# First g and v products by pairs of token tiles, with the parameters turned among them, in a one-core hybrid encoder kernel

## The reference, cut to what matters

```python
xn = rms_norm(x, pre_g)                          # per token, gain pre_g
u  = einsum('btd,de->bte', xn, w_in)             # 1024 -> 5120 columns
xr, gr, cv_v, cv_g, gc = split(u, 5)             # 1024 columns each: x, gr, v, g, gc below
xr = causal_dwconv(xr, rg_buf, rg_cw, rg_cb)     # width 4
hr = rg_lru(xr, rg_h, wa, ba, wx, bx, lam)       # gates, then h = a*h + b over the tokens
y_r = hr * silu(gr)
v  = cv_v * sigmoid(cv_g)                        # the first thing made from u: g, then v
v  = causal_dwconv(v, cv_buf, cv_cw, cv_cb)      # width 31
v  = silu(layer_norm(v, cv_lg, cv_lb))
y_c = (einsum(v, cv_w2) + cv_b2) * silu(gc)
y  = einsum(concat([y_r, y_c]), w_out)           # 2048 -> 1024
out = x + rms_norm(y, post_g)
```

## Time and profile before

| what | value |
|---|---|
| median of the runs | 809.05 us |
| span of the profiled execution, first to last instruction | 806.3 us |
| TensorE busy (PE) | 783.2 us, 97% |
| VectorE busy (DVE) | 665.5 us, 83% |
| ScalarE busy (ACT) | 422.1 us, 52% |
| GpSimd busy (POOL) | 384.9 us, 48% |
| DMA engines | 32.5% on the main queue |

### The profile page before, as it was taken

How to read it: one execution, slowest core, us unless ns; L and a number is a source line. 1 busy time by engine, 2 the same in 40 slices (tenths; PEclk the granted TensorE clock), 3 DMA queues, 4 the chain that set the end, 5 groups by cost and what they waited for, 6 DMA issues and landing times. The chain is left out here.

```text
span 806.3 us, 12690 instructions
## 1 busy us (share of the span) xinstructions
PE 783.2 (97%) x5158; PEld 763.0 (95%) x5158; DVE 665.5 (83%) x564; ACT 422.1 (52%) x657; POOL 384.9 (48%) x215
## 2 busy tenths in 40 slices
PE   5999999999999999999999999999999799999996
PEld 4899999999999999999999989999999799999995
DVE  5589999999998986986995988982438899799894
ACT  6522374474474365365366379953515244566652
POOL 4325347346546446456556744010036896389220
PEclk9999999999999999999999999999999999999998
DMA  8311211211211121121121120423279463554683
GB/s 269 96 54 37 70 53 53 80 52 53 73 59 52 58 73 52 53 79 52 53 79 52 53 80 27 134 71 116 80 240 279 142 171 107 157 157 132 187 262 139
DMA packets 111404, 82.37 MB, mean 102 GB/s; under 512 B 3179, under 2 KB 101483, under 8 KB 111362
## 3 DMA queue, kind: packets, MB, share of 16 engines
q1 hardware_dynamic: 110432, 80.68, 32.5%
q0 software_dynamic: 928, 1.12, 0.6%
q10 hardware_dynamic: 2, 0.00, 0.0%
HBM read 68.55 MB, written 13.25 MB: 101 GB/s over the span
## 5 line engine op out<-in xcount | busy, mean ns | idle before, releaser
L919 PE MATMUL ps<-act_hi,w_hi 128*128 128x352 f32 (+4 forms) x1384 | 445.1, 322 | 5.6 <-DVE w_lo L2067 4.2
L921 PE MATMUL ps<-act_hi,w_lo 128*128 128x352 f32 (+4 forms) x1384 | 438.6, 317 | 0.0
L920 PE MATMUL ps<-act_lo,w_hi 128*128 128x352 f32 (+3 forms) x1320 | 420.2, 318 | 0.0
L1870 DVE SCALAR_TENSOR_TENSOR ps<-cv_in,par_cv,ps 128x1086 f32<-128x1086 f32 x232 | 313.9, 1353 | 7.8
L919 PEld LDWEIGHTS ps<-act_hi,w_hi 128*128 128x128 f32 x1384 | 260.5, 188 | 12.7 <-issue 7.2
L921 PEld LDWEIGHTS ps<-act_hi,w_lo 128*128 128x128 f32 x1384 | 261.1, 189 | 0.0
L920 PEld LDWEIGHTS ps<-act_lo,w_hi 128*128 128x128 f32 x1320 | 248.1, 188 | 0.2
L721 POOL TENSOR_TENSOR w_lo<-wstage,w_hi 128x1024 fp32r<-128x1024 f32 x40 | 97.3, 2447 | 74.7 <-ACT w_hi L1272 74.6
L920 PE MATMUL ps<-act_hi,w_hi 128*128 128x264 f32 (+2 forms) x256 | 73.7, 288 | 0.0
L1272 ACT ACTIVATE w_hi<-wstage 128x1024 fp32r<-128x1024 f32 x47 | 48.6, 1052 | 22.4 <-PE ps L921 15.4
L919 PE MATMUL ps<-act_lo,w_hi 128*128 128x264 f32 x192 | 55.5, 289 | 0.0
(11 more groups left out here) (241 smaller groups left out, 1048.5 us busy)
## 6 DMA issues: line engine op xcount, KB each, us to landing
wstage<-in_w_in SPq DMA_DIRECT2D x40, 512.0 KB, 3.9
wstage<-in_w_out SPq DMA_DIRECT2D x20, 512.0 KB, 5.0
w_stage<-in_w_out SPq DMA_DIRECT2D x19, 512.0 KB, 5.0
stage<-in_w_out SPq DMA_DIRECT2D x9, 512.0 KB, 4.1
silu_spill<-silu_gc SPq DMA_DIRECT2D x8, 528.0 KB, 2.7
yr_spill<-y_rg SPq DMA_DIRECT2D x8, 528.0 KB, 2.8
silu_l<-silu_spill SPq DMA_DIRECT2D x8, 528.0 KB, 3.7
yr<-yr_spill SPq DMA_DIRECT2D x2, 2112.0 KB, 11.1
```

What stands on the lines that cost most here:

```text
L919: pe.matmul(out, wh, xh, start=start, stop=False)
L920: pe.matmul(out, wh, xl, start=False, stop=False)
L921: return pe.matmul(out, wl, xh, start=False, stop=stop)
L1870: STT(out=acc, in0=src, scalar=w, in1=acc, op0=ALU.mult, op1=ALU.add).then_inc(taps, 1)
```

## The change

Section g of the first tile is no longer done in three chunks over 358, 358 and 356 tokens, but in four parts over 256, 256, 256 and 304 tokens (`FIRST_G`; the first two share one bank). The first chunk of v stands between the second and the third part of g. The turns of token tiles 4 to 8 stand at other steps. The parameters are turned ahead of g's last part. POOL makes both parts of the second weight block, ahead of the parameter loads. The gain row is copied once by DVE from PSUM to SBUF, and the norms of token tiles 4 to 8 read it there, which frees PSUM banks 6 and 7. TensorE does twelve products of the identity by a constant into banks that nobody reads (`keep_busy`), three, two, one and six, ahead of the turns of tiles 0 to 3. ACT's table for tanh and exp is loaded ahead of the first tanh, and the first tanh and the first v input are taken in smaller pieces.

```diff
@@ -82,9 +82,11 @@
 BANK = {"g": [2, 3, 4], "v": [0, 1, 2], "gr": [3, 4, 0], "x": [1, 2, 3], "gc": [4, 0, 1]}
 GATE_BANK = [(4, 0), (0, 1), (1, 2)]
 ACC_BANK = 5
-FIRST_BANK = {"g": [4, 5, 6], "v": [1, 2, 3]}
+FIRST_BANK = {"g": [6, 4, 5], "v": [7, 2, 3]}
+FIRST_G = [(0, 4 * P), (4 * P, 2 * P), (6 * P, T - 6 * P)]
 X_BANK = [0, 2, 4, 0, 2, 0, 2, 0, 2]
 GAIN_BANK = 6
+PSUM_GAINS = 4
 
 
 LAST_BANK = {"gr6": [2, 3, 4], "x": [2, 3, 4], "gc": [0, 1, 5], "gr": [0, 1, 6]}
@@ -295,6 +297,7 @@
     assert 4 * D <= 4 * R_LEN
     par_rows = at("par_rows", [D], F32, arena)
     sq_junk = at("sq_junk", [D], F32, arena + 4 * R_LEN)
+    gain = at("gain", [D], F32, arena + 2 * 4 * R_LEN)
 
 
 
@@ -373,6 +376,7 @@
         g_loaded = sem("g_loaded")
         ones_set = sem("ones_set")
         gain_spread = sem("gain_spread")
+        gain_set = sem("gain_set")
         par_loaded = sem("par_loaded")
         gatew_loaded = sem("gatew_loaded")
         consts = sem("consts")
@@ -818,9 +822,10 @@
                     pool.dma_start(par_rows[row:row + src.shape[0], :], src).then_inc(par_loaded, 16)
 
 
-            pool.wait_ge(w_loaded[0], 16)
-            pool.tensor_copy(WHI[0], wstage[:, 0]).then_inc(w_his, 1)
-            w_lo_part(0, 0, 1)
+            for slot in range(2):
+                pool.wait_ge(w_loaded[slot], 16)
+                pool.tensor_copy(WHI[slot], wstage[:, slot]).then_inc(w_his, 1)
+                w_lo_part(slot, slot, slot + 1)
             load_par(par_src)
 
 
@@ -832,7 +837,6 @@
                 for b in range(2):
                     pool.dma_start(gate_w[64 * b:64 * b + 64, (m + b) % 2],
                                    w[0].rearrange("(c b) i j -> b i c j", b=2)[b]).then_inc(gatew_loaded, 16)
-            w_lo_part(1, 1, 2)
 
             pool.wait_ge(par_turned, 1)
             pool.memset(rg_in[:, 0:RPAD], 0.0).then_inc(pads, 1)
@@ -920,7 +924,17 @@
                 pe.matmul(out, wh, xl, start=False, stop=False)
                 return pe.matmul(out, wl, xh, start=False, stop=stop)
 
-            def chunk(s, j, bank=None, between={}):
+            def first_part(s, bank, b0, c0, n, between={}):
+
+                w = WSLOT[s]
+                for k in range(KT):
+                    mm = product(ps[:, bank, b0:b0 + n], WHI[w][:, k], WLO[w][:, k],
+                                 act_hi[:, k, c0:c0 + n], act_lo[:, k, c0:c0 + n], k == 0, k == KT - 1)
+                    if k in between:
+                        turn_x(between[k])
+                return mm
+
+            def chunk(s, j, bank=None):
 
                 bank = BANK[s][j] if bank is None else bank
                 c0, n = (META + j * OCH, OCH) if s in ("gr", "gc") else XCH[j]
@@ -928,8 +942,6 @@
                 for k in range(KT):
                     mm = product(ps[:, bank, 0:n], WHI[w][:, k], WLO[w][:, k],
                                  act_hi[:, k, c0:c0 + n], act_lo[:, k, c0:c0 + n], k == 0, k == KT - 1)
-                    if k in between:
-                        turn_x(between[k])
                 mm.then_inc(proj, 1)
 
             def turn_x(t):
@@ -1030,22 +1042,42 @@
                                start=True, stop=True)
             mm.then_inc(gain_spread, 1)
             pe.wait_ge(consts, 5)
-            for t in range(4):
-                turn_x(t)
+            def keep_busy(bank, n):
+
+                for _ in range(n):
+                    pe.matmul(ps[:, bank, 0:P], ident[:, :], mean_w[:, :], start=True, stop=True)
+
+            keep_busy(4, 3)
+            turn_x(0)
+            keep_busy(4, 2)
+            turn_x(1)
+            keep_busy(4, 1)
+            turn_x(2)
+            pe.wait_ge(x_lo, 1)
+            keep_busy(0, 6)
+            turn_x(3)
+            pe.wait_ge(gain_set, 1)
+            bank = FIRST_BANK["g"]
             pe.wait_ge(w_los, 1)
-            for j, between in enumerate(({0: 4, 2: 5, 5: 6}, {1: 8}, {})):
-                if j == 1:
-                    turn_x(7)
-                pe.wait_ge(x_lo, 3 * j + 3)
-                chunk("g", j, FIRST_BANK["g"][j], between=between)
+            pe.wait_ge(x_lo, 2)
+            first_part("g", bank[0], 0, 0, 2 * P)
+            turn_x(4)
+            pe.wait_ge(x_lo, 4)
+            first_part("g", bank[0], 2 * P, 2 * P, 2 * P, {3: 5}).then_inc(proj, 1)
+            pe.wait_ge(w_los, 2)
+            first_part("v", FIRST_BANK["v"][0], 0, *XCH[0], {1: 6, 6: 7}).then_inc(proj, 1)
+            pe.wait_ge(x_lo, 6)
+            first_part("g", bank[1], 0, *FIRST_G[1], {0: 8}).then_inc(proj, 1)
 
             pe.wait_ge(par_loaded, 16 * (len(par_src) + 2))
+            pe.wait_ge(x_lo, 8)
             for k in range(KT):
-                mm = pe.transpose(ps[:, 7 * (k // 4), k % 4 * P:k % 4 * P + PAR],
+                mm = pe.transpose(ps[:, k // 4, k % 4 * P:k % 4 * P + PAR],
                                   par_rows[0:PAR, k * P:(k + 1) * P], ident[0:PAR, 0:PAR])
             mm.then_inc(par_turned, 1)
-            pe.wait_ge(w_los, 2)
-            for j in range(3):
+            pe.wait_ge(x_lo, NX)
+            first_part("g", bank[2], 0, *FIRST_G[2]).then_inc(proj, 1)
+            for j in range(1, 3):
                 chunk("v", j, FIRST_BANK["v"][j])
             tile(0, True)
             with pe.Fori(1, KT - 1) as c:
@@ -1304,25 +1336,33 @@
                 x_stats(t)
                 x_hi_part(t - 1)
             x_hi_part(NX - 1)
-            act.wait_ge(w_los, 1)
-            act.wait_ge(w_loaded[1], 16)
-            w_hi_part(1, 1)
+            def first_tanh(j, done):
+                c0, n = FIRST_G[j]
+                act.wait_ge(proj, done)
+                return A(tanh_g[:, c0:c0 + n], ps[:, FIRST_BANK["g"][j], 0:n], ACT.Tanh, scale=0.5)
+
+            act.preload_act_table(ACT.Exp)
+            first_tanh(0, 1)
+            first_tanh(1, 3).then_inc(g_read, 1)
             act.wait_ge(par_turned, 1)
             for i in range(2):
                 A(par[:, 4 * i:4 * i + 4, 0:PAR],
-                  ps[:, 7 * i, :].rearrange("p (k n) -> p k n", n=P)[:, :, 0:PAR], ACT.Copy).then_inc(par_ready, 1)
+                  ps[:, i, :].rearrange("p (k n) -> p k n", n=P)[:, :, 0:PAR], ACT.Copy).then_inc(par_ready, 1)
 
             act.wait_ge(der, 2)
             A(small[:, 1, :], small[:, 1, :], ACT.Exp, scale=-1.0).then_inc(der_exp, 1)
+            act.wait_ge(w_los, 2)
+            act.wait_ge(w_loaded[0], 32)
+            act.wait_ge(proj, 4)
+            w_hi_part(0, 0)
+            first_tanh(2, 4).then_inc(g_read, 1)
 
             def gate_tanh(d):
 
-                fst = isinstance(d, int) and d == 0
-                n = 0 if fst else 6 if isinstance(d, int) and d == 1 else d * (3 * NS) - 12
-                bank = (FIRST_BANK if fst else BANK)["g"][0]
+                n = 6 if isinstance(d, int) and d == 1 else d * (3 * NS) - 12
+                bank = BANK["g"][0]
                 act.wait_ge(proj, n + 2)
-                if not fst:
-                    act.wait_ge(glu_done, 2 * d)
+                act.wait_ge(glu_done, 2 * d)
                 A(tanh_g[:, 0:716].rearrange("p (j n) -> p j n", j=2), ps[:, bank:bank + 2, 0:358], ACT.Tanh,
                   scale=0.5).then_inc(g_read, 1)
                 act.wait_ge(proj, n + 3)
@@ -1529,9 +1569,6 @@
                 act.wait_ge(proj, n + 15)
                 silu_pair(silu_gc[:, OCH:TO], BANK["gc"][1], gc_read)
 
-            gate_tanh(0)
-            act.wait_ge(w_loaded[0], 32)
-            w_hi_part(0, 0)
             act.wait_ge(pads, 3)
             act.wait_ge(der, DER_STEPS)
             cv_setup(0, 0, False)
@@ -1796,11 +1833,16 @@
                 dve.wait_ge(x_rs, t + 1)
                 if t == 0:
                     dve.wait_ge(gain_spread, 1)
+                if t == PSUM_GAINS:
+                    dve.wait_ge(gain_set, 1)
+                if t < PSUM_GAINS:
+                    gains = ps[0:rows, GAIN_BANK:GAIN_BANK + 2, :].rearrange("p b n -> p (b n)")
+                else:
+                    gains = gain[0:rows, :]
                 if t >= 3:
                     dve.wait_ge(x_turned, t - 2)
                 STT(out=x_norm[0:rows, t % 3, :], in0=x_in[0:rows, t % 4, :], scalar=sums[0:rows, t:t + 1],
-                    in1=ps[0:rows, GAIN_BANK:GAIN_BANK + 2, :].rearrange("p b n -> p (b n)"), op0=ALU.mult,
-                    op1=ALU.mult).then_inc(x_normed, 1)
+                    in1=gains, op0=ALU.mult, op1=ALU.mult).then_inc(x_normed, 1)
 
             def x_lo_part(t):
                 rows = x_rows[t]
@@ -1810,7 +1852,10 @@
                 TT(act_lo[:, :, t * P:t * P + rows], src, act_hi[:, :, t * P:t * P + rows],
                    ALU.subtract).then_inc(x_lo, 1)
 
-            for t in range(3):
+            x_norm_part(0)
+            dve.tensor_copy(gain[:, :].rearrange("p (b n) -> p b n", b=2), ps[:, GAIN_BANK:GAIN_BANK + 2, :])\
+                .then_inc(gain_set, 1)
+            for t in range(1, 3):
                 x_norm_part(t)
```

(5 more changed lines are left out.)

## The result

The changed kernel takes 803.60 us (median of four runs, 803.52 to 804.01) where the kernel before takes 808.53 in the runs beside it (four, 806.60 to 809.57): ratio 0.9939, 95% interval 0.9927 to 0.9951. Repeated with five runs on another occasion it is 804.42 against 808.84, 0.9944 (0.9930 to 0.9958). Direction and mechanism were right, the size was not: 1.5 us have to be explained.

What follows compares the result with a forecast made beforehand. TensorE was taken to bound the kernel; 4.0 us out of its opening turn the profiled 806.3 into 802.3, and 2.75 us from span to median give 805.1 us, range 803.6 to 808.0.

Steps and rivals of the forecast that it cites:

- Idle to be had: First tile's g and v in the opening: of TensorE's 32.9 us, 28.0 are work and 4.5 idle.
- parts of g: First tile's g: 24 extra products cost nothing, 11.7 us either way; 0.116 us per 256-token product, 0.138 for 304.
- walk: TensorE's opening step by step from 16.85 to v's end at 45.4 instead of 49.45: gain 4.0 us, bounds 3.0 to 4.5.
- The start: First g product waits for two low parts, not three, and starts at 16.85: 1.2 us of the 4.5 idle.
- The sum: Whole kernel: 4.0 us off profiled 806.3 gives 802.3; plus 2.75 from span to median of runs, 805.1.
- Identity products: Ahead of the turns of tiles 0 to 3: cost nothing at the higher clock; 0.47 us each at the lower.
- The rival of the lower clock: TensorE at 1.2 GHz at tile 3's turn, 2.4 us late: 807.3 us (chance 0.03) or beyond 810.7 (0.06).
- Gain row's copy: DVE's PSUM copy behind norm 0: 1.2 us, hidden where DVE sat idle 1.48 us, so costing nothing.
- late parameters: Rival, opening: 5.1 us of blocked descriptor writing plus 2 of traffic make TensorE stand 2.9 us; 808.0 us, chance 0.07.
- norm 4: DVE's norm of token tile 4, two SBUF sources: at most 0.3 us lost beside POOL's second subtraction, inside cover.
- Convolution and what follows: Behind v: constants ready by 43, convolution moves along with TensorE, first tap near 46.4, DVE keeps its distance.
- given back: Rival, output stage: the end of TensorE's 3.9 us wait does not follow TensorE; time near 809, chance 0.10.

Runs made afterwards that it cites:

- the six products alone: Kernel before with only six identity products ahead of the turn of token tile 3: 808.82 us, ratio 0.9997.
- the parameters late: Changed kernel with the parameters turned behind g's last part, where they stood before: 804.96 us, ratio 0.9951.
- identity-only kernels: Kernel before plus only identity products: all twelve at the change's places, 808.10 us (0.9991), or only six ahead of tile 3's turn, 808.82 us (0.9997).
- fill run: Kernel before with only 16 identity products added in the output stage, meant to fill TensorE's wait: 811.55 us, ratio 1.0038.

## Why the prediction was right, and where it was not

**Idle to be had, parts of g, walk.** Right. 28.65 us were measured for the 28.55 worked out, and the profile has no wait of TensorE in it; the 304-token product costs 0.139 (21 of them from 33.60 to 36.52), 0.138 was taken. v between is worth 1.6 us (forecast in the expectation 2.0) and the start by two tiles 3.9, with what the clock costs in it.

**The start.** Two terms of the forecast failed by their size. This is the first: 16.85 was forecast for the first g product, 15.87 and 15.79 came. The distance to tile 3 was right, and it moves one for one with that tile's landing; but the landing was read from one execution in which it came 1 us later than in the other profiles (12.61 against 11.27 to 11.71 with the loads in this order, 11.96 once). In the kernel before, an early landing brought less, since the clock then fell, in three of three profiles: its first tap lies between 49.9 and 51.2 whether tile 3 comes at 11.3 or at 12.6. In the changed kernel nothing stands between landing and gain. So the kernel before hid a second cost that its profile didn't show.

**The sum.** This is the second mis-sized term, as large as the first: the 2.75 us put around the span. In the four executions of the kernel after the time lies 1.76 to 1.84 above the span, 803.56 and 801.8 in the profiled one. The 2.75 was the median of some executions less the span of another. It may have been wrong for that execution too, which would then have taken about 808.1 us; but this is not known. In 93 executions of the kernel before whose span is on record the distance is 1.74 to 2.95 and above 2.3 in 16 of them, one with the span 806.3 and the time 809.13 among these; in 108 executions of all other versions it is 1.74 to 1.92. Why only the kernel before has these long distances is open.

So 1.0 us comes from the start and 1.0 from the distance; 0.1 was lost in the walk and 0.4 behind the output stage's wait, which leaves the 1.5. The forecast span, 802.3, was only 0.5 off because the last two hid half of the first, which is luck.

**Identity products.** Free, as said. At the lower level two of them from 9.72 to 10.57 are 0.43 each from start to start, where 0.47 was worked out; the six from 13.12 to 14.64 are 0.25. The reason given, that the level had risen because of unbroken work, is not needed: without them the first g product follows tile 3's turn by the same 1.2 us. The rival of the lower clock had the mechanism on the wrong kernel: not the changed one ran slow behind its turns, the one before did, in three of four profiles.

**Gain row's copy, POOL, late parameters.** The copy took 1.22 us in DVE's gap. The parameters' last issue was at 24.2 and landed 4.5 later, 28.7 (forecast 29.5), and TensorE took them at 32.73 without a wait. POOL's issues beside the two-source norms took 0.49 to 0.53 us, as they did in the kernel before (0.48 to 0.53), so the blocked descriptors that the prediction weighed from the Trainium skill, "SBUF — State Buffer", did not occur here. The box it drew on names DVE operations in a two-port mode as those that lock POOL out; in which mode the norms ran no run shows. What the prediction underrated is norm 4: its bound of 0.3 us held only because POOL ended in time.

**Convolution and what follows.** The first tap moved by 4.9 with TensorE, and from it to the end are 756.4 and 756.8 us in the kernel after against 755.9, 756.6 and 756.3 before. Nothing was given back up to 624 us. Behind it the distance to the end scatters from 177.2 to 179.6 between the profiles of kernels that have the same work there (179.6 with the six products alone, 178.9 with the parameters late), and the 0.4 of the first pair lies within that. What makes this scatter is open.

Open too is why the time of the identity-only kernels fell by 0.2 and 0.7 us where their openings show 1.3. In the profile with six products the gain is still whole at the output stage's wait (it ends at 627.96, against 628.58 to 629.85 in the kernel before and its fill run) and is gone behind it.

## What to carry to other kernels

Before the span of one profiled execution is turned into a forecast of the median, that execution's own time is needed, and the landings that its critical start hangs on want a second profile. A short wait of TensorE in front of dense work can be paid twice, by the wait and by the clock; work that is ready closes both, filler at best the second, and where DVE and POOL are the bound even that brings nothing. To find what bounds a long stretch, delay one engine and see which distance stays: here it was the one from the end of v to the output stage's wait. When a load is moved forward, look at what moves back on POOL, and whether DVE then runs an operation with two SBUF sources beside it.

## What the runs showed of the hardware

In three of four openings of the kernel before, with waits of 0.9 to 1.4 us ahead of eight transposes and of 1.26 behind them, TensorE's granted clock fell to 0.50 for 3 to 7 us; in the fourth, with 0.71 and 1.26, it held. With six or twelve identity products it held in two of two, and with twelve and one wait of 1.15 us behind the transposes (g's first part as one chunk) it fell. The versions with the start by two tiles held 1.00 in ten of ten, one of them without any identity product. In the first 14 us the granted clock is given as 1.00 while the transposes run at 0.21 us apiece, twice their later time: there only durations tell the level. A DVE operation of 1.28 us with two SBUF sources took 3.07 beside a POOL subtraction of 2.40. 3.73 us of extra TensorE work in a stage that DVE and POOL fill cost 2.2 to 3.0 by the medians. And the time of an execution lay 1.74 to 2.95 us above its span in the kernel before, 1.74 to 1.92 in every other version.
